# Two transformer blocks on one core: the first squares, one merge, the key-norm sums and two bias loads put at other places in their queues

## The chip, the cores and the metric

The kernel runs on one core of a Trainium2 chip. The metric is the time that one execution takes on the device, in microseconds (us), as the median of three runs. The engines are called as in the profile: PE (TensorE, the matmuls), PEld (its weight loads), DVE (VectorE), ACT (ScalarE), POOL (GpSimd) and SP (SyncE, which here only issues the weight transfers). The engines run side by side, each through its own list of instructions in order, and semaphores tie them together: `wait_ge(s, n)` holds an engine until the semaphore `s` has reached `n`, `then_inc` raises it when an instruction is done.

## What is computed

`reference()` sends 256 tokens of width 1024 through `first_block` and then `second_block`. Cut to the four places that matter here:

```python
y = xf * lax.rsqrt(jnp.mean(xf * xf, axis=-1, keepdims=True) + NORM_EPS)   # rms_norm, then * gain

# first_block, layer 0: gated linear attention (gla_mixer), 4 heads, causal, with a decay per channel
attn = jnp.einsum('bhid,bhjd,bhijd->bhij', qi, ki, decay)
o = rms_norm(o, head_gain) * jax.nn.silu(g)

# first_block, layer 1: differential attention; the keys are normed per half head
kv = rms_norm(h, kv_norm) @ w_kv
k = rms_norm(k.reshape(B, S, DIFF_HEADS, 2, DIFF_DH), k_norm)

# second_block: three branches; the state-space one (ssd) ends in a norm per group of 512 channels,
# the sliding-window attention adds a bias that depends on the distance of two tokens
y = rms_norm_2((y * jax.nn.silu(z)).reshape(b, l, SSD_GROUPS, SSD_INNER // SSD_GROUPS), norm_g)
logits = logits + rel_bias
```

## The kernel before

All matrix products are float32 products made out of parts. A chunk is 128 columns of a weight (all 1024 rows); there are 420 chunks, and SP fetches two at a time (a slab of 1 MB) into a ring of four. ACT copies a chunk rounded into `w_hi` (`cut_hi`, L1199), DVE puts the rest into `w_lo` (`cut_lo`, L1926). The activations are split in the same way into `X.hi` (ACT), `X.lo` (DVE, `operand_lo`, L1939 and L1941) and a bfloat16 copy `X.bf`. PE then takes 16 products of the high weight with the high and the low activation (L469, L470) and 8 of the low weight with the bfloat16 copy (L479). Chunks are cut three ahead (`AHEAD`), and everything is written out by hand: the order of a list is the order of the code in the engine's block. So what comes first where is decided by the loops below alone.

Four places are touched.

**The start.** ACT makes the eight high operands of the first norm's input, DVE the eight low ones. At the same time POOL runs `first_squares`: four squares of pairs (L2679), three sums (L2683) and a last one into `sumsq` (L2686). PE runs chunk 0 and chunk 1 as each low operand comes, then chunk 2, and then `stats(0, ...)` (L557, L560), which needs `sumsq`; the chunk results wait for the scale that comes of it.

**The end of the linear attention.** In a loop over `u`, DVE runs `decayed(u - 1)` (L2077 to L2082, the factors of a unit, from the exponentials of ACT at L1367) and then `merge(u - 2)` (L2090 and L2091, the masked sum of the scores that PE made of the unit before). PE's `scores(7)` (L645, L647) waits for both `decayed(7)` and `merge(6)`.

**The key norms.** Eight chunks (C_DK is 96) make the keys, one head each. For head n: DVE scales it (L1945), ACT squares it (`head_sq`, L1225), PE sums the squares (`head_sums`, L570), ACT turns the sum into a scale (`head_rstd`, L1229 and L1233) and DVE applies it (`head_out`, L1971). PE takes the sum of head n - 1 right behind chunk n.

**The bias loads.** The state-space branch ends in `ssd_norm` (L2414), which raises `s_on`. POOL waits for the last of these, then issues the loads of the bias for the first two units of the window attention (`bias`, L2760), then waits for the operands of the next product and issues the load of `mem` (L2781). DVE's `swa_max` (L2543) needs the bias; ACT's `swa_exp` (L1799) comes behind it, and in ACT's list the square of the next query head (L1695), for which PE's sum (L570) waits.

Of the kernel before, what the change touches and what calls it, by code (L numbers as in the profile page):

```python
# [25 lines left out]
KC = D // P  # L26
# [4 lines left out]
GLA_HEADS, GLA_RANK, GLA_TAU = 4, 16, 16.0  # L31
DIFF_HEADS, DIFF_DH = 8, 64
LAMBDA_INIT = 0.8 - 0.6 * float(np.exp(-0.3))
TAPS, SSD_TAPS = 31, 4
SSD_HEADS, SSD_GROUPS = 32, 4
# [116 lines left out]
def program(nc, w_d, par_d, con_d, gm_d, x_d, mem_d, band_d, out_d):  # L152
    ctx = ExitStack()
    with ctx:
# [41 lines left out]
        XA, XB = XSet("xa"), XSet("xb")  # L196
# [6 lines left out]
        def pcol(name, i=0, n=1):  # L203
            return par[:, PCOL[name] + i:PCOL[name] + i + n]
# [6 lines left out]
        class Cut:  # L211
# [5 lines left out]
            def __call__(self, *shape, rows=P):  # L217
# [6 lines left out]
                if len(shape) == 3:  # L224
# [35 lines left out]
        d_k, d_q = cut(DIFF_HEADS, T), cut(DIFF_HEADS, T)  # L260
# [90 lines left out]
        sa = {n: sem("s_" + n) for n in ("tap", "silu", "z", "dtf", "dts", "dt", "dtx", "dta", "dte", "da", "cs", "bias", "x", "xd", "cb", "cbs", "c", "e",  # L351
                                         "sc", "y", "yd", "sq", "n", "r", "on", "eb", "nx", "gb")}
# [99 lines left out]
        def _(pe):  # L452
# [110 lines left out]
            def head_sums(k):  # L563

                pe.wait_ge(hn_sq, k + 1)
                if k >= 2:
                    pe.wait_ge(hn_ln, k - 1)
                if DIFF_HEADS < k < 2 * DIFF_HEADS or k == HN_K + 1:
                    pe.wait_ge(hn_ln, k)
                mm(head_sums_at(k), bones, hn_sqb[:, k % 2], start=True, stop=True).then_inc(hn_mm, 1)  # L570
# [44 lines left out]
            n = GLA_RANK + 1  # L615
# [110 lines left out]
            for n in range(9):  # L726
                if n == 0:
                    opening_chunk(C_DK, 0, XA, XA_DIFF, C_DK - 8)
                elif n < 8:
                    chunk(C_DK + n, n, XA, None)  # L730
                    if n == 1:
                        stats(2, True, True)
                if n:
                    head_sums(n - 1)

            mm(ps[0:SWA_HEADS, 7, 0:BAND], par[0:33, PCOL["rel"]:PCOL["rel"] + SWA_HEADS], con[0:33, CCOL["oh"]:CCOL["oh"] + BAND],
               start=True, stop=True).then_inc(band_mm, 1)
# [1 line left out]
            def v_or_q(i):  # L739

                if i < 2 * DIFF_HEADS:
                    c = C_DVQ + i
                    if i in Q_AT:
                        chunk(c, c, XB, XB_DQ if i == 0 else None, banks=2)
                    else:
                        token_half(c, XA, None, banks=2)
                if i - 1 in Q_AT:
                    head_sums(DIFF_HEADS + Q_AT.index(i - 1))
# [38 lines left out]

            for i in range(DVQ_AHEAD):
                v_or_q(i)
            pe.wait_ge(bf_set, 2)  # L790
            pe.wait_ge(band_set, 1)
            diff_scores(0)
# [200 lines left out]
            for s in range(R_END):  # L993
                g, i = (s - R_LEAD) // R_GROUP, (s - R_LEAD) % R_GROUP
# [179 lines left out]
        def _(act):  # L1174
# [52 lines left out]
            def head_rstd(k):  # L1227
                act.wait_ge(hn_mm, k + 1)
                A(lnt[:, k % 2], head_sums_at(k), ACT.Ln, bias=eps[:, 0:1], scale=1.0 / 64).then_inc(hn_ln, 1)  # L1229
                act.wait_ge(hn_ln, k + 1)  # L1230
                if k >= 2:
                    act.wait_ge(hn_out, k - 1)
                A(hn_rb[:, k % 2], lnt[:, k % 2], ACT.Exp, scale=-0.5).then_inc(hn_r, 1)  # L1233
# [163 lines left out]
            for n in range(9):  # L1397
                if n < 7:
                    cut_hi(C_DK + n + 1 + AHEAD, C_DK + n + 1 + AHEAD)
                if n == 0:  # L1400
                    rms(2, rstd, rtok)
                if n < 8:
                    A(XB.hi[:, n], H[:, n], ACT.Copy, scale=pcol("b_norm", n)).then_inc(XB.hi_done, 1)
                    head_sq(n, C_DK + n, d_k[:, n])
                if n:
                    head_rstd(n - 1)

            act.wait_ge(da["lam"], 1)
            A(d_lam[:, 2:4], d_lam[:, 0:2], ACT.Exp).then_inc(da["lame"], 1)
# [14 lines left out]
            def v_or_q(i):  # L1424

                c = C_DVQ + i + AHEAD
                if i in Q_AT:
                    cut_hi(c, c)
                elif i % 2 == 0:
                    cut_hi(c, c)  # L1430
                    diff_value(i)
                elif i < 2 * DIFF_HEADS:
                    diff_value(i)
                    cut_hi(c, c)
# [29 lines left out]
            def diff_exp(u):  # L1464
                t = u % 2
                act.wait_ge(da["max"], u + 1)
                if u >= 2:
                    act.wait_ge(da["a"], u - 1)
                for c in range(2):
                    ins = A(d_p[:, u % 2, c, 0:(t + 1) * P], diff_scores_at()[:, c, 0:(t + 1) * P], ACT.Exp,  # L1470
                            bias=d_st[:, u % 2, c:c + 1], accum_out=d_st[:, u % 2, 2 + c:3 + c])
                ins.then_inc(da["p"], 1)

            for i in range(DVQ_AHEAD):
                q_norm(i)
                v_or_q(i)
            diff_exp(0)
            for u in range(2 * DIFF_HEADS):
                h, t = u // 2, u % 2
# [217 lines left out]
            for s in range(R_END):  # L1697
                cut_hi(C_R + s + AHEAD, C_R + s + AHEAD)
                g, i = (s - R_LEAD) // R_GROUP, (s - R_LEAD) % R_GROUP
# [210 lines left out]
        def _(dve):  # L1910
# [57 lines left out]
            def head_out(k, x, gain):  # L1968

                dve.wait_ge(hn_r, k + 1)  # L1970
                STT(x, x, gain, hn_rb[:, k % 2], ALU.mult, ALU.mult).then_inc(hn_out, 1)  # L1971
# [133 lines left out]
                    operand_lo(XB, KC * XB_GLA + 2 * h + half + 1, 2 * h + half, g_og[:, h % 2, half], pcol("a_head_norm", half))  # L2105

            for u in range(2 * GLA_HEADS + 2):
                if 1 <= u <= 2 * GLA_HEADS:
                    decayed(u - 1)
                if u >= 2:  # L2110
                    merge(u - 2)
                if u in (6, 7):
                    gated(u - 6)
                if u < 2 * GLA_HEADS:
                    for c in (8 + 2 * u, 9 + 2 * u):
                        cut_lo(c + AHEAD, c + AHEAD)
                        if c < C_GV:
                            scaled(c, c, g_gate[:, c - C_GG], 2)
                if u == 7:
                    out_lo(0)  # L2120
# [34 lines left out]
            for n in range(10):  # L2155
                if n < 8:
                    cut_lo(C_DK + n + AHEAD, C_DK + n + AHEAD)
                    if n == 0:
                        dve.wait_ge(rstd_done, 3)
                    scaled(C_DK + n, n, d_k[:, n])  # L2160
                    operand_lo(XB, KC * XB_DQ + n + 1, n, H[:, n], pcol("b_norm", n))
                if n >= 2:
                    head_out(n - 2, d_k[:, n - 2], pcol("k_norm"))

            def v_or_q(i):

                if i - 1 in Q_AT:
                    c = C_DVQ + i - 1
                    dve.wait_ge(bank_free, c)
                    scaled(c, c, d_q[:, Q_AT.index(i - 1)], banks=2)  # L2170
                if 0 < i < 2 * DIFF_HEADS:
                    c = C_DVQ + i + AHEAD - 1
                    cut_lo(c, c)

            def q_out(i):

                if i - 3 in Q_AT:
                    h = Q_AT.index(i - 3)
                    head_out(DIFF_HEADS + h, d_q[:, h], gains[:, 2:3])

            for i in range(DVQ_AHEAD):
                v_or_q(i)
                q_out(i)

            dve.wait_ge(da["lame"], 1)
# [28 lines left out]
            for u in range(2 * DIFF_HEADS):  # L2214
# [12 lines left out]
                if u in DIFF_OPERAND_AT:  # L2227
                    i = DIFF_OPERAND_AT[u]
# [60 lines left out]
            for n in range(16):  # L2289
                c = C_CONV + n  # L2290
                i = n // 2
# [361 lines left out]
        def _(pool):  # L2653
# [19 lines left out]

            def first_squares():

                for i in range(4):
                    pool.wait_ge(in_done[i // 2], 16)
                    h = H[:, 2 * i:2 * i + 2]
                    G.tensor_tensor(x_squares[:, min(i, 1)], h, h, ALU.mult).then_inc(sq_step, 1)  # L2679
                    steps[0] += 1  # L2680
                    if i:
                        pool.wait_ge(sq_step, steps[0])
                        G.tensor_tensor(x_squares[:, 0], x_squares[:, 0], x_squares[:, 1], ALU.add).then_inc(sq_step, 1)  # L2683
                        steps[0] += 1
                        pool.wait_ge(sq_step, steps[0])
                G.tensor_tensor(sumsq[:], x_squares[:, 0, 0:T], x_squares[:, 0, T:2 * T], ALU.add).then_inc(sq_step, 2 * KC - 1 - steps[0])  # L2686
                steps[0] = 2 * KC - 1
# [60 lines left out]
                pool.wait_ge(ca["silu"], k + 1)  # L2748
                G.tensor_scalar(XA.bf[:, k], c_out[:, k], one[:, 0:1], None, ALU.mult).then_inc(XA.bf_done, 1)

            pool.wait_ge(sa["on"], 4 * SSD_GROUPS)

            def bias(u):

                p, t = u // 2, u % 2
                nk = (t + 1) * P
                if u >= 2:
                    pool.wait_ge(wa["ss"], u - 1)
                skew = bass.AP(band_d.tensor, 2 * p * BAND + P - 1 + (1 - t) * P, [[SWA_HEADS * BAND - 1, P], [BAND, 2], [1, nk]])
                pool.dma_start(w_bias[:, u % 2, :, 0:nk], skew).then_inc(band_in[u % 2], 16)  # L2760
# [15 lines left out]

            bias(0)
            bias(1)
            pool.wait_ge(XB.bf_done, KC * (XB_Y0 + 1))
            pool.wait_ge(XB.lo_done, KC * (XB_Y0 + 1))  # L2780
            pool.dma_start(x_mem, mem_d).then_inc(mem_in, 16)  # L2781
# [153 lines left out]
```

## Time and profile before

| | |
|---|---|
| median of three runs | 1421.48 us (1421.24 to 1424.57) |
| the profiled execution | 1420.15 us, of which 1418.1 us lie between its first and last instruction |
| PE busy | 1367.4 us, 96% of the span |
| PEld busy | 1260.7 us, 89% |
| DVE busy | 1044.8 us, 74% |
| ACT busy | 890.8 us, 63% |
| POOL busy | 335.1 us, 24% |
| mean granted PE clock | 0.993 of full speed |
| moved from and to memory | 233.8 MB, 165 GB/s on the mean |

The profile is one execution, seen instruction by instruction. Its time is 1.33 us below the median of the runs. A busy share is an average over a program with many stages, so it says who is loaded most, and not what a given stage waits for. That is read from the view of waits (an engine, the line that it could not start, and who released it) and from the timeline of an engine, where each row gives the start, the time taken, the engine, the line, the operation, what it writes and reads, how many alike were merged into the row, and in brackets how long the engine had been idle and what ended that.

### The profile page before, as it was taken

To read this page: it belongs to the slowest core of one execution; us is meant where nothing else is said; L and a number is where in the kernel's file an instruction comes from. 1 tells how busy PE (TensorE), PEld (TensorE's weight loads), DVE (VectorE), ACT (ScalarE), POOL (GpSimd) and SP (SyncE) were. 2 spreads that over 40 slices of the span, in tenths; PEclk is the share of its full clock that TensorE was granted. 3 is DMA by queue.
4 is the path that set the end of the run, shared out by engine and by line. 5 is a ranking of instruction groups with operands and counts; after the bars stand their busy time and mean duration, and the time that the engine had idled before them with its cause. 6 is when DMAs were issued, how large, how long until landed. Compare 5 with 4: busy or idle time off the path is not lost.

```text
span 1418.1 us, 29905 instructions
## 1 busy us (share of the span) xinstructions
PE 1367.4 (96%) x11462; PEld 1260.7 (89%) x11462; DVE 1044.8 (74%) x1570; ACT 890.8 (63%) x1689; POOL 335.1 (24%) x326
## 2 busy tenths in 40 slices
PE   6998999999999999999899999999999999999998
PEld 6997999998888999999888989888788899899998
DVE  6797855567577865568999999867797686666554
ACT  5555744457577554467887878848667565655543
POOL 2000410115001210032855535410411031411110
PEclk9999999999999999999999999999999999999999
DMA  8332565554843555554444444434455454356551
GB/s 321 135 120 90 180 207 182 203 183 146 195 135 118 195 193 195 191 179 161 166 149 150 149 157 142 155 114 138 158 176 176 138 198 149 114 184 199 187 202 66
DMA packets 35608, 233.80 MB, mean 165 GB/s; under 512 B 4000, under 2 KB 7072, under 8 KB 8352
## 3 DMA queue, kind: packets, MB, share of 16 engines
q1 hardware_dynamic: 31104, 223.75, 45.9%
q10 hardware_dynamic: 3216, 4.19, 1.9%
q0 software_dynamic: 1168, 4.20, 1.0%
q8 instruction: 83, 1.36, 0.4%
q14 instruction: 37, 0.30, 0.1%
HBM read 227.93 MB, written 4.19 MB: 164 GB/s over the span
## 4 chain that ended last, share of the span: by engine, by line
PE 75%; DVE 16%; ACT 4%; issue 3%; DMA 0%; DVEq 0%; ACTq 0%; SPq 0%
PE ps L469 12%; PE ps L470 11%; PE ps L479 11%; PE ps L538 7%; PE ps L539 6%; PE ps L544 6%; DVE w_lo L1926 5%; DVE arena L2346 2%; PE ps L880 2%; PE ps L881 2%; PE ps L884 2%; DVE xa_both L1941 2%; PE ps L521 2%; PE ps L522 1%; PE ps L524 1%
## 5 line engine op out<-in xcount | busy, mean ns | idle before, releaser
L1926 DVE TENSOR_TENSOR w_lo<-raw,w_hi 128x1024 bf16<-128x1024 f32 x420 | 548.3, 1308 | 202.1 <-ACT w_hi L1199 201.8
L1199 ACT CAST w_hi<-raw 128x1024 fp32r<-128x1024 f32 x420 | 438.5, 1047 | 304.0 <-PE ps L544 133.8
L469 PE MATMUL ps<-xa_both,w_hi 128*128 128x256 f32 x1296 | 326.3, 293 | 12.0 <-ACT w_hi L1199 10.3
L470 PE MATMUL ps<-xa_both,w_hi 128*128 128x256 f32 x1296 | 309.1, 280 | 0.0
L469 PEld LDWEIGHTS ps<-xa_both,w_hi 128*128 128x128 f32 x1296 | 247.2, 191 | 18.3 <-issue 12.0
L470 PEld LDWEIGHTS ps<-xa_both,w_hi 128*128 128x128 f32 x1296 | 247.7, 191 | 0.5
L538 PE MATMUL ps<-xb_both,w_hi 128*128 128x256 f32 x832 | 204.7, 289 | 0.0
L539 PE MATMUL ps<-xb_both,w_hi 128*128 128x256 f32 x832 | 195.2, 277 | 0.0
L479 PE MATMUL ps<-xa_bf,w_lo 128*128 128x256 bf16 x1296 | 169.4, 274 | 1.2 <-DVE w_lo L1926 1.1
L2705 POOL TENSOR_TENSOR arena<-arena 128x256 f32<-128x256 f32 x96 | 69.7, 727 | 388.7 <-DVE arena L2008 388.7
L538 PEld LDWEIGHTS ps<-xb_both,w_hi 128*128 128x128 f32 x832 | 156.6, 188 | 1.6 <-DVE xb_both L1941 0.2
L539 PEld LDWEIGHTS ps<-xb_both,w_hi 128*128 128x128 f32 x832 | 156.7, 188 | 0.1
L880 PE MATMUL ps<-xb_both,w_hi 128*128 128x256 f32 x592 | 148.0, 293 | 4.4 <-DVE arena L2346 3.0
L881 PE MATMUL ps<-xb_both,w_hi 128*128 128x256 f32 x592 | 139.0, 278 | 0.0
L479 PEld LDWEIGHTS ps<-xa_bf,w_lo 128*128 128x128 bf16 x1296 | 113.8, 98 | 18.6 <-DVE w_lo L1926 2.0
L880 PEld LDWEIGHTS ps<-xb_both,w_hi 128*128 128x128 f32 x592 | 111.4, 188 | 8.2 <-issue 5.9
L881 PEld LDWEIGHTS ps<-xb_both,w_hi 128*128 128x128 f32 x592 | 111.5, 188 | 0.6
L544 PE MATMUL ps<-xb_bf,w_lo 128*128 128x256 bf16 x832 | 108.9, 274 | 0.0
L544 PEld LDWEIGHTS ps<-xb_bf,w_lo 128*128 128x128 bf16 x832 | 73.0, 98 | 10.6
L469 PE MATMUL ps<-xb_both,w_hi 128*128 128x256 f32 x320 | 80.2, 292 | 0.5 <-DVE xb_both L1939 0.4
L884 PE MATMUL ps<-xb_bf,w_lo 128*128 128x256 bf16 x592 | 77.5, 274 | 0.0
L470 PE MATMUL ps<-xb_both,w_hi 128*128 128x256 f32 x320 | 75.8, 279 | 0.0
(350 smaller groups left out, 2368.2 us busy)
## 6 DMA issues: line engine op xcount, KB each, us to landing
raw<-weights SPq DMA_DIRECT2D x210, 1024.0 KB, 4.9
band<-arena ACTq DMA_DIRECT2D x1, 3072.0 KB, 35.6
arena<-band POOLq DMA_DIRECT2D x8, 256.0 KB, 3.2
arena<-gla_masks SPq DMA_DIRECT2D x1, 1088.0 KB, 15.2
H<-x_t SPq DMA_DIRECT2D x2, 512.0 KB, 4.6
arena<-band POOLq DMA_DIRECT2D x8, 128.0 KB, 2.7
arena<-mem_t POOLq DMA_DIRECT2D x1, 1024.0 KB, 5.9
out_t<-H ACTq DMA_DIRECT2D x8, 128.0 KB, 2.0
```

Of the source, the lines that this page charges most:

```text
L469: mm(ps[:, bank, 0:T], w_hi[:, s, k], X.hi[:, k], start=k == 0, stop=False)
L470: mm(ps[:, bank, 0:T], w_hi[:, s, k], X.lo[:, k], start=False, stop=False)
L479: last = mm(ps[:, bank, 0:T], w_lo[:, s, k], X.bf[:, k], start=False, stop=k == KC - 1)
L538: mm(sums(n), w_hi[:, s, i], X.hi[:, k], start=opens, stop=False)
L539: mm(sums(n), w_hi[:, s, i], X.lo[:, k], start=False, stop=False)
L544: done = mm(sums(n), w_lo[:, s, i], X.bf[:, k], start=False, stop=last and (k, n) == DOWN[j][-1] and j >= 4)
L880: mm(ps[:, bank, 0:T], w_hi[:, c % HI_SLOTS, k], XB.hi[:, k], start=k == 0, stop=False)
L881: mm(ps[:, bank, 0:T], w_hi[:, c % HI_SLOTS, k], XB.lo[:, k], start=False, stop=False)
L884: last = mm(ps[:, bank, 0:T], w_lo[:, c % HI_SLOTS, k], XB.bf[:, k], start=False, stop=k == KC - 1)
L1199: nc.scalar.copy(w_hi[:, j % HI_SLOTS].rearrange("p k n -> p (k n)"), raw[:, j // 2 % RING, j % 2]).then_inc(hi_done, 1)
L1926: TT(w_lo[:, j % HI_SLOTS].rearrange("p k n -> p (k n)"), raw[:, j // 2 % RING, j % 2], w_hi[:, j % HI_SLOTS].rearrange("p k n -> p (k n)" ...
L2705: G.tensor_tensor(m_sq[:, j % 2], m_relu[:, j % 2], m_relu[:, j % 2], ALU.mult).then_inc(sq_done, 1)
```

## The change

It moves waits and instructions; no arithmetic is added or left out. POOL's first squares wait until DVE has written all eight low operands. In the last step but one of the linear attention's loop DVE merges unit 6 before it makes the factors of unit 7. In the key loop the sum of head n - 2 instead of head n - 1 follows chunk n on PE, the scale on ACT and its use on DVE move with it, and the last head's sum, scale and use go behind the first query chunk. POOL's wait for the last `ssd_norm` is put behind the first two bias loads, which now wait for the last products and weighted scores of the state-space branch instead.

```diff
             # PE
-                if n:
-                    head_sums(n - 1)
+                if n >= 2:
+                    head_sums(n - 2)
...
             for i in range(DVQ_AHEAD):
                 v_or_q(i)
+                if i == 0:
+                    head_sums(DIFF_HEADS - 1)
...
             # ACT
-                if n:
-                    head_rstd(n - 1)
+                if n >= 2:
+                    head_rstd(n - 2)
...
                 q_norm(i)
                 v_or_q(i)
+                if i == 0:
+                    head_rstd(DIFF_HEADS - 1)
...
             # DVE
             for u in range(2 * GLA_HEADS + 2):
+                if u == 2 * GLA_HEADS:
+                    merge(u - 2)
                 if 1 <= u <= 2 * GLA_HEADS:
                     decayed(u - 1)
-                if u >= 2:
+                if u >= 2 and u != 2 * GLA_HEADS:
                     merge(u - 2)
...
-                if n >= 2:
-                    head_out(n - 2, d_k[:, n - 2], pcol("k_norm"))
+                if n >= 3:
+                    head_out(n - 3, d_k[:, n - 3], pcol("k_norm"))
...
                 v_or_q(i)
+                if i == 1:
+                    head_out(DIFF_HEADS - 1, d_k[:, DIFF_HEADS - 1], pcol("k_norm"))
                 q_out(i)
...
             # POOL
             def first_squares():
+                pool.wait_ge(XA.lo_done, KC)
...
-            pool.wait_ge(sa["on"], 4 * SSD_GROUPS)
+            pool.wait_ge(sa["y"], 2 * SSD_GROUPS)
+            pool.wait_ge(sa["sc"], 4 * SSD_GROUPS)
...
             bias(0)
             bias(1)
+            pool.wait_ge(sa["on"], 4 * SSD_GROUPS)
             pool.wait_ge(XB.bf_done, KC * (XB_Y0 + 1))
```

How the lists stand afterwards, at three places. First PE at the key chunks: L557 and L560 are the row statistics behind key chunk 1, L570 is a head's sum, L469 and L470 open the next chunk. Between the two versions the list differs here by one row:

```order
 L557 MATMUL ps<-sumsq,ones 128x256
 L560 MATMUL ps<-ones,sumsq 128x1 x2
-L570 MATMUL ps<-hn_sqb,con 128x256
 L469 MATMUL ps<-xa_both,w_hi 128x256
 L470 MATMUL ps<-xa_both,w_hi 128x256
```

and it comes back behind the first query chunk (`xb` operands):

```order
 L470 MATMUL ps<-xb_both,w_hi 128x256
 L479 MATMUL ps<-xb_bf,w_lo 128x256 x8
+L570 MATMUL ps<-hn_sqb,con 128x256
 L469 MATMUL ps<-xb_both,w_hi 128x256
 L470 MATMUL ps<-xb_both,w_hi 128x256
```

So chunk 2 follows the statistics at once, each later place of a sum holds the sum of one head earlier, and one sum stands behind the first query chunk.

Second DVE at the end of the linear attention, before (L2077 to L2082 make the factors of unit 7, the first L2090 and L2091 merge unit 6, the second unit 7):

```order
L1941 SCALAR_TENSOR_TENSOR xb_both<-arena,par,xb_both 128x256 [waits xb_hi_done] x2
L2077 TENSOR_TENSOR arena<-arena 128x896 [waits g_e]
L2081 TENSOR_TENSOR arena<-arena 128x128
L2082 TENSOR_TENSOR arena<-arena 128x896
L2090 TENSOR_TENSOR arena<-ps,arena 128x1024 [waits g_m,g_s]
L2091 TENSOR_REDUCE arena<-arena 128x128 [waits dve_step]
L2090 TENSOR_TENSOR arena<-ps,arena 128x1024 [waits g_m,g_s]
```

and in the changed kernel, whose lines stand four further down here (L2094 is the L2090 of before):

```order
L1945 SCALAR_TENSOR_TENSOR xb_both<-arena,par,xb_both 128x256 [waits xb_hi_done] x2
L2094 TENSOR_TENSOR arena<-ps,arena 128x1024 [waits g_m,g_s]
L2095 TENSOR_REDUCE arena<-arena 128x128 [waits dve_step]
L2081 TENSOR_TENSOR arena<-arena 128x896 [waits g_e]
L2085 TENSOR_TENSOR arena<-arena 128x128
L2086 TENSOR_TENSOR arena<-arena 128x896
L2094 TENSOR_TENSOR arena<-ps,arena 128x1024 [waits g_m,g_s]
```

The merge of unit 6 has moved ahead of the three instructions that wait for ACT's exponentials (`g_e`).

Third POOL before the window attention, before (`s_on` is the last norm, `w_ss` the biased scores):

```order
L2749 TENSOR_SCALAR xa_bf<-arena,one 128x256 [waits c_silu] x3
L2760 DMA arena<-band 128x2x128 [waits s_on]
L2760 DMA arena<-band 128x2x256
L2781 DMA arena<-mem_t 128x2048 [waits xb_lo_done,xb_bf_done]
L2760 DMA arena<-band 128x2x128 [waits w_ss]
```

and in the changed kernel:

```order
L2758 TENSOR_SCALAR xa_bf<-arena,one 128x256 [waits c_silu] x3
L2770 DMA arena<-band 128x2x128 [waits s_sc,s_y]
L2770 DMA arena<-band 128x2x256
L2792 DMA arena<-mem_t 128x2048 [waits xb_lo_done,xb_bf_done,s_on]
L2770 DMA arena<-band 128x2x128 [waits w_ss]
```

The order of the transfers is the same; the wait for `s_on` has moved from the first of them to the third.

## Rows read from the trace of the kernel before

**Rows 1.** The page, chain that ended last: shares of the span by engine.

```profile
PE 75%; DVE 16%; ACT 4%; issue 3%; DMA 0%; DVEq 0%; ACTq 0%; SPq 0%
```

**Rows 2.** Waits of PE, whole span: us in total, times, longest us.

```profile
PE ps L570 <- ACT hn_sqb L1225: 3.0, 2, 2.2
```

**Rows 3.** Stretches: us, busy time (count) per engine, granted PE clock, DMA share, GB/s.

```profile
117.70:124.50 6.80, 5.26 (x22) 5.02 (x23) 2.83 (x3) 1.14 (x2) 0.00 (x0) 0.50 0.00 0
336.20:339.60 3.40, 3.40 (x17) 3.32 (x16) 2.44 (x4) 1.98 (x5) 3.40 (x3) 0.50 0.78 294
1005.30:1008.60 3.30, 3.30 (x12) 2.00 (x12) 2.91 (x9) 2.32 (x7) 1.26 (x2) 0.50 0.11 15
```

**Rows 4.** Timeline of the start: DVE, POOL, ACT, PE.

```profile
6.00 9.42 DVE L1941 SCALAR_TENSOR_TENSOR xa_both<-H,par,xa_both 128x256 fp32r<-128x256 f32 x8 [6.00 <-ACT xa_both L1285]
15.35 3.48 DVE L1926 TENSOR_TENSOR w_lo<-raw,w_hi 128x1024 bf16<-128x1024 f32 x3
...
5.44 2.22 POOL L2679 TENSOR_TENSOR arena<-H 128x512 f32<-128x512 f32 x2 [4.20 <-DMA H<-x_t]
14.41 0.73 POOL L2686 TENSOR_TENSOR sumsq<-arena 128x256 f32<-128x256 f32 x1
...
9.13 1.99 ACT L1199 CAST w_hi<-raw 128x1024 fp32r<-128x1024 f32 x2 [0.38 <-DMA raw<-weights]
...
10.28 0.55 PE L469 MATMUL ps<-xa_both,w_hi 128*128 128x256 f32 x1 [10.28 <-ACT w_hi L1199]
16.07 0.42 PE L469 MATMUL ps<-xa_both,w_hi 128*128 128x256 f32 x1
18.63 0.35 PE L469 MATMUL ps<-xa_both,w_hi 128*128 128x256 f32 x1
23.66 0.60 PE L557 MATMUL ps<-sumsq,ones 128*128 128x256 f32 x2
```

**Rows 5.** Timeline of POOL further on: one product beside DVE's work, one later.

```profile
1013.80 1.41 POOL L2771 TENSOR_TENSOR sqtmp<-arena 128x256 f32<-128x256 f32 x1
...
1024.22 0.61 POOL L2771 TENSOR_TENSOR sqtmp<-arena 128x256 f32<-128x256 f32 x1
```

**Rows 6.** Timeline of DVE and PE at the end of the linear attention.

```profile
111.62 1.66 DVE L1941 SCALAR_TENSOR_TENSOR xb_both<-arena,par,xb_both 128x256 fp32r<-128x256 f32 x2 [0.36 <-ACT xb_both L1351]
113.73 1.09 DVE L2077 TENSOR_TENSOR arena<-arena 128x896 f32<-128x896 f32 x1 [0.44 <-ACT arena L1367]
...
115.94 1.22 DVE L2090 TENSOR_TENSOR arena<-ps,arena 128x1024 f32<-128x1024 f32 x1
117.19 1.91 DVE L2091 TENSOR_REDUCE arena<-arena 128x128 f32<-128x1024 f32 x1
...
112.06 0.39 PE L647 MATMUL ps<-arena 128*128 128x128 f32 x2
...
119.24 3.33 PE L645 MATMUL ps<-arena 128*128 128x128 f32 x14 [3.83 <-DVE arena L2091]
```

**Rows 7.** Timeline of PE and ACT at the key chunks.

```profile
335.69 0.75 PE L570 MATMUL ps<-hn_sqb,con 128*128 128x256 f32 x2 [2.23 <-ACT hn_sqb L1225]
...
340.53 0.60 PE L570 MATMUL ps<-hn_sqb,con 128*128 128x256 f32 x2
...
343.74 0.60 PE L570 MATMUL ps<-hn_sqb,con 128*128 128x256 f32 x2
...
335.22 0.42 ACT L1225 ACTIVATE hn_sqb<-arena 128x256 f32<-128x256 f32 x1 [0.16 <-DVE arena L1945]
```

**Rows 8.** Timeline of PE, POOL and DVE at the first bias loads.

```profile
978.74 0.44 PE L954 MATMUL ps<-con,arena 128*64 128x128 f32 x4
...
999.22 1.62 POOL L2760 DMA_DIRECT2D arena<-band  x2 [42.33 <-DVE arena L2414]
...
1002.04 0.43 DVE L2543 SCALAR_TENSOR_TENSOR arena<-ps,arena 128x256 f32<-128x256 f32 x1 [0.93 <-DMA arena<-band]
...
1005.07 1.11 PE L570 MATMUL ps<-hn_sqb,con 128*128 128x256 f32 x2 [2.72 <-ACT hn_sqb L1695]
```

## The prediction

> **What bounds the kernel now.** I read the chain that ended last first: three quarters of it are PE's own work [rows 1], so time can only be won where PE stands still or runs at the lower clock. Next come the waits of PE, where the reader looks for the lines that the change touches: the key heads' sums (L570, released by ACT's L1225) cost 3.0 us in two waits, the longer 2.2 [rows 2]; the others stand in brackets in the timelines. Third, the granted clock by stretches. Three of these four places are followed, or one is filled, by a stretch at 0.50, which is 1.2 instead of 2.4 GHz: 6.8 us at the end of the linear attention, 3.4 at the key chunks, 3.3 at the bias loads [rows 3]. A wait there costs its length and then some more. Last, the timelines of the four places, for who is late.
>
> **The squares at the start.** DVE's eight low operands end at 15.42, 9.42 us for eight, and POOL's chain runs from 5.44 to 15.14 at the same time [rows 4]. PE's first 16 matmuls go from 10.28 to 16.07, 5.79 us, since most of them wait for a low operand; the next twelve go from 16.07 to 18.63, 0.213 each, and 16 at that pace are 3.41 [rows 4]. So 2.4 us are lost there, and PE could be at the statistics (23.66) at 21.3 at best. In the change POOL starts when the low operands are done. ACT's high halves, which they need, end at 8.75 (the cast behind them starts at 9.13 after 0.38 of idle time [rows 4]). Elsewhere two low operands take 1.66 us, 0.83 each [rows 6], so the last is done by 9.6; with POOL silent it should be quicker, and I take 9.4, an estimate.
>
> What is then late is the squares themselves: PE's L557 needs `sumsq`. From 9.4, POOL needs its old 9.7 us and now meets DVE's four splits of the weights (1.16 each [rows 4]), because the first casts are done at 11.1 [rows 4]. A POOL product beside such a split took 1.41 and without one 0.61 [rows 5], 0.8 more; four of these make 3.2. So the squares end at 9.4 + 9.7 + 3.2 = 22.3, and the statistics run at 22.3 instead of 23.66: **1.4 gained**. Bounds: without any slowing the squares end at 19.1, PE decides, and it is 2.4. If POOL stands for the whole of the four splits and the small one behind them, some 1.2 each, they end at 25.1 and 1.4 are lost. I take the middle, by the row that shows just this pair of engines.
>
> The rule that speaks against this edit is in the Trainium skill, "SBUF — State Buffer", section "SBUF: two separate sides": a VectorE operation with two inputs in SBUF and a GpSimd operation that reads SBUF lock each other out, and whichever starts first keeps the shared ports for its whole instruction. The trace agrees as to the direction [rows 5]. By that rule each split holds POOL back for its full length, which is the bound of 25.1 and a loss of 1.4; by the rows' pace it is 22.3.
>
> **One merge first.** DVE is free at 113.28 (111.62 + 1.66), and idles 0.44 until ACT's exponentials let L2077 start at 113.73; the scores of unit 6 that the merge needs are done at 112.45 [rows 6]. In the new order the merge (115.94 to 119.10, 3.16) starts at once, and the factors (113.73 to 115.94, 2.21) follow it without a wait, their exponentials being done by then. PE's L645 then starts at 113.28 + 3.16 + 2.21 = 118.65 instead of 119.24, some of which is the semaphore's way: I take **0.5 gained**. PE stays idle for 3.3 us. The low stretch of 6.8 us is twice as long as the two others [rows 3], and PE works through only its last 5.3 us. If PE's earlier return ended it at the others' length, the 3.4 us that fall away give half of that, 1.7, back; so the bounds are 0 and 2.2.
>
> **The key sums one chunk later.** The first sum waits 2.23 and starts at 335.69, when ACT's square (335.22 + 0.42) is just done [rows 7]. Now chunk 2 runs in that time, about 333.3 to 336.1, and its sum finds the square done at 335.64. The 2.23 go, and so does the reason for the low clock from 336.2 to 339.6 [rows 3]: from 335.69 to 340.53, one sum and one chunk take 4.84 us, the next sum and chunk to 343.74 take 3.21 [rows 7], which is 1.63 more. The second wait (3.0 - 2.2 = 0.8 [rows 2]) belongs to the last head, whose sum moves behind the first query chunk; it goes too. Together 2.2 + 1.6 + 0.8: **4.7 gained**. The moved scale on ACT and the use on DVE run under PE's next chunk, 2.8 us, in which each has one cast or split and three small steps. If the clock falls all the same, 3.0 are left; the upper bound is 5.0, as the 0.3 of the sum itself also moves out of the slow stretch.
>
> **The bias loads.** POOL issues them at 999.22, after a wait of 42.33 for DVE's norm; the last product of the state-space branch that they now need ends at 979.18 (978.74 + 0.44) [rows 8]. Nothing of POOL stands between, and the load of `mem` behind them keeps its old wait. The bias is then there long before DVE's `swa_max`, which now starts 0.93 late, at 1002.04 [rows 8]. The instructions up to PE's L570 at 1005.07 hang on it one by one, so its wait of 2.72 becomes 1.8: **1.0 gained**, with the 0.93 rounded up. What is late next is ACT's square, behind the exponentials in its list. If the shorter wait no longer brings the clock down (1005.3 to 1008.6 at 0.50 [rows 3]), up to half of these 3.3 us comes on top, 2.6 in all; if DVE's other work takes the gap, nothing is gained.
>
> **Sum.** 1.4 + 0.5 + 4.7 + 1.0 = 7.6 us off the profiled execution of 1420.15, so 1412.55. That execution stands 1.33 below the median of 1421.48, so against the median the forecast is **1413.9**. No edit adds an instruction, and what follows each place hangs on semaphores, so it comes earlier with it.
>
> **Rivals.** A measurement of this kernel can tell 0.3% from no change, which is 4.3 us: faster means under 1417.2.
>
> *The squares become the late wait.* POOL is held back fully; the start loses 1.4 instead of gaining it: -4.8, 1416.7. For it: DVE's splits come one behind another there. Against: 1.41 and not 1.8 in [rows 5].
>
> *The clock gives more.* The start is bound by PE (2.4), the stretch at 119 gets shorter (2.2), the one at 1005 goes (2.6): with 4.7 it is -11.9, 1409.6; half of the extra gives 1411.7. For it: all three low stretches follow PE waits that get shorter. Against: two of these waits stay at 1.8 and 3.3 us.
>
> *Low clocks stay and the small ones miss.* The clock at the key chunks still falls (3.0), the start and the merge give nothing, the bias 1.0: -4.0, 1417.5, no change. It includes that the change doesn't do what it says at the start or at the merge.
>
> *Slower, by the clock.* Each low stretch of 3.4 us costs 1.63 [rows 7]. All later waits of PE shift by up to 7.6 us, and short ones that left the clock up may then bring it down. From five new stretches on (7.6 / 1.63 = 4.7) the gain is gone; with eight (13.0) it is 5.4 slower, 1426.9. Against: the waits are not longer than before, and only their place in time shifts.
>
> **How the numbers follow.** Forecast 0.56, more from the clock 0.22, late squares 0.12, no change 0.07, slower 0.03. The range takes in the first three and leaves the last two out: from 1409.5, just under the whole of the extra, to 1417.0, just over the late squares. Faster is 0.56 + 0.22 + 0.12 = 0.90, same 0.07, slower 0.03.
>
> **What would show it.** The low operands end by about 9.5 and `sumsq` near 22.3; if it ends after 23.7, the first step is wrong. L645 starts some 6.2 us after the last L647 of the unit before ends, where it was 6.8 (112.45 to 119.24). No wait of L570 for L1225 is left and the clock stays at 1.00 at the key chunks; a new wait at a sum, or a cast that comes late, would break the largest step. `swa_max` no longer waits for a DMA, and L570 behind it waits about 1.8. If all four are seen and the time is not near 1413.9, then waits behind them have grown, and the step "comes earlier with it" is the wrong one.

## The result, and the profile after

The changed kernel takes 1411.56 us (median of 5 runs, 1410.91 to 1414.28), the kernel before 1421.48. The ratio is 0.9926, with a 95% interval from 0.9916 to 0.9937: 9.9 us or 0.74% faster. The forecast was 1413.9 with a range from 1409.5 to 1417.0, so range and direction held, and 2.3 us were won that the sum did not have. Between the two profiled executions the sum is nearly met: it said 1412.55 there, and 1412.25 was measured. The forecast took over the distance of 1.33 between the profile of before and its median; the changed kernel's profile lies 0.69 above its own median, and the two distances make up 2.0 of the 2.3.

First the waits of PE in the changed kernel (us in total, times, longest):

```profile
PE ps L570 <- ACT hn_sqb L1699: 3.4, 2, 1.7
PE ps L645 <- DVE arena L2086: 3.2, 1, 3.2
PE ps L557 <- POOL sumsq L2695: 1.7, 1, 1.7
PE ps L758 <- ACT arena L1472: 1.5, 1, 1.5
PE ps L1088 <- DVE arena L2566: 1.3, 2, 0.9
```

The key sums' waits of [rows 2] have no row any more. The wait at the bias loads fell from 2.72 [rows 8] to 1.7 (the other 1.7 of the first row is the untouched one at 960), and that of L645 from 3.83 [rows 6] to 3.2. One wait is new: PE stands 1.7 us for the squares. The wait of L758 is the old one, and will matter below.

Then the timeline of the changed kernel at the four places, in the columns of the rows above; lines are numbered up to 11 higher here:

```profile
5.98 3.28 DVE L1945 SCALAR_TENSOR_TENSOR xa_both<-H,par,xa_both 128x256 fp32r<-128x256 f32 x8 [5.98 <-ACT xa_both L1287]
...
9.34 3.02 POOL L2688 TENSOR_TENSOR arena<-H 128x512 f32<-128x512 f32 x2 [8.10 <-DVE xa_both L1945]
12.44 2.14 POOL L2692 TENSOR_TENSOR arena<-arena 128x512 f32<-128x512 f32 x1
21.42 0.72 POOL L2695 TENSOR_TENSOR sumsq<-arena 128x256 f32<-128x256 f32 x1
...
13.84 0.41 PE L469 MATMUL ps<-xa_both,w_hi 128*128 128x256 f32 x1
14.23 0.28 PE L469 MATMUL ps<-xa_both,w_hi 128*128 128x256 f32 x1
22.20 0.70 PE L557 MATMUL ps<-sumsq,ones 128*128 128x256 f32 x2 [1.72 <-POOL sumsq L2695]
...
110.74 0.39 PE L647 MATMUL ps<-arena 128*128 128x128 f32 x2
117.29 3.36 PE L645 MATMUL ps<-arena 128*128 128x128 f32 x14 [3.20 <-DVE arena L2086]
...
334.55 0.60 PE L570 MATMUL ps<-hn_sqb,con 128*128 128x256 f32 x2
337.70 0.60 PE L570 MATMUL ps<-hn_sqb,con 128*128 128x256 f32 x2
...
971.75 1.62 POOL L2770 DMA_DIRECT2D arena<-band  x2 [22.67 <-PE ps L956]
...
996.25 0.70 PE L570 MATMUL ps<-hn_sqb,con 128*128 128x256 f32 x2 [1.68 <-ACT hn_sqb L1699]
```

The low operands are done at 9.26 and the squares at 22.14, so the statistics run 1.46 us earlier than in [rows 4]. The key sums follow one another in 3.15 us from the first on, where the first pair was 4.84 apart [rows 7]. The bias loads go out 27 us earlier than in [rows 8].

Last the stretches, in the columns of [rows 3]:

```profile
116.60:123.40 6.80, 6.11 (x24) 5.75 (x25) 2.89 (x3) 1.07 (x3) 0.00 (x0) 0.50 0.01 2
331.80:337.60 5.80, 5.80 (x51) 5.52 (x51) 5.79 (x10) 5.29 (x12) 5.80 (x4) 1.00 0.91 340
372.90:376.30 3.40, 3.38 (x27) 2.80 (x28) 3.22 (x10) 1.98 (x8) 0.00 (x0) 1.00 1.02 419
997.30:1000.60 3.30, 2.90 (x15) 2.38 (x12) 3.23 (x9) 2.17 (x7) 1.26 (x2) 0.50 0.29 60
```

The stretches behind the merge and behind the bias loads are still at 0.50. The key chunks run at 1.00. The third row is a place that the prediction did not look at: right behind L758's wait of 1.5 us. In the kernel before, the same piece of the program stood at 0.50:

```profile
380.60:384.00 3.40, 3.40 (x17) 3.33 (x16) 3.03 (x7) 3.06 (x9) 0.00 (x0) 0.50 1.02 422
```

Where the gain comes from can be read by pairing the products of both kernels one by one and taking the difference of their starts. The changed kernel is 1.4 us ahead behind the statistics, 1.6 after the linear attention, 6.0 at the second key sum, 6.6 behind the last one, 8.1 at 384 us of the kernel before, 8.6 behind the bias loads, 8.3 some 20 us later and 8.0 at the end. The profiled executions are 7.9 apart (1420.15 and 1412.25); the medians 9.9. In these two executions the key sums and L758 give 6.5 where the sum had 4.7 for the key sums, and smaller losses at the other places use up most of that surplus.

### The profile page after: what moved, and what is told of

Read it like the earlier page. It is cut to its first block, busy times and chain, and to the rows that moved or that the text cites. A ratio compares the mean times of both kernels' runs of the same rounds, so it can differ in the third digit from the quotient of the medians.

```text
span 1410.2 us, 29907 instructions
## 1 busy us (share of the span) xinstructions
PE 1362.8 (97%) x11462; PEld 1257.2 (89%) x11462; DVE 1042.2 (74%) x1570; ACT 890.7 (63%) x1689; POOL 338.6 (24%) x326
## 4 chain that ended last, share of the span: by engine, by line
PE 75%; DVE 16%; ACT 4%; issue 3%; POOL 1%; DMA 0%; DVEq 0%; ACTq 0%; SPq 0%; POOLq 0%
PE ps L469 12%; PE ps L470 11%; PE ps L479 11%; PE ps L538 7%; PE ps L539 6%; PE ps L544 6%; DVE w_lo L1930 5%; DVE arena L2354 2%; PE ps L882 2%; PE ps L883 2%; PE ps L886 2%; PE ps L521 1%; PE ps L522 1%; PE ps L524 1%; DVE xa_both L1945 1%
## 5 line engine op out<-in xcount | busy, mean ns | idle before, releaser
L469 PE MATMUL ps<-xa_both,w_hi 128*128 128x256 f32 x1296 | 323.2, 291 | 10.9 <-ACT w_hi L1201 10.3
L470 PE MATMUL ps<-xa_both,w_hi 128*128 128x256 f32 x1296 | 306.5, 278 | 0.0
L469 PEld LDWEIGHTS ps<-xa_both,w_hi 128*128 128x128 f32 x1296 | 245.5, 189 | 16.4 <-issue 12.0
L470 PEld LDWEIGHTS ps<-xa_both,w_hi 128*128 128x128 f32 x1296 | 245.5, 189 | 0.5
L469 PE MATMUL ps<-xb_both,w_hi 128*128 128x256 f32 x320 | 81.0, 294 | 0.5 <-DVE xb_both L1943 0.4
L470 PE MATMUL ps<-xb_both,w_hi 128*128 128x256 f32 x320 | 76.5, 280 | 0.0
```

Of the source, the lines that this page charges most:

```text
L469: mm(ps[:, bank, 0:T], w_hi[:, s, k], X.hi[:, k], start=k == 0, stop=False)
L470: mm(ps[:, bank, 0:T], w_hi[:, s, k], X.lo[:, k], start=False, stop=False)
```

## The experiments

**Each edit alone.** What is to be told apart is whether the extra belongs to one edit or to chance. The four edits, cut to the line that says them:

```diff
 # only_squares
             def first_squares():
+                pool.wait_ge(XA.lo_done, KC)
 # only_merge
+                if u == 2 * GLA_HEADS:
+                    merge(u - 2)
 # only_keys
-                if n:
-                    head_sums(n - 1)
+                if n >= 2:
+                    head_sums(n - 2)
 # only_bias
-            pool.wait_ge(sa["on"], 4 * SSD_GROUPS)
+            pool.wait_ge(sa["y"], 2 * SSD_GROUPS)
+            pool.wait_ge(sa["sc"], 4 * SSD_GROUPS)
...
             bias(1)
+            pool.wait_ge(sa["on"], 4 * SSD_GROUPS)
```

> Only the first edit: POOL's squares start behind the eight low operands. Theory A (each edit is worth its own wait and the low-clock stretch right behind it, and the 2.3 us beyond the forecast are chance of the clock elsewhere): statistics at about 22.2 instead of 23.7, a gain of 1.4, so some 1420.1 us. Theory B (an edit also takes low-clock stretches away further on, by moving later waits in time): 1 to 2 us more than that in the median, 1418 to 1419. Rival of the first step: if the exclusion by the weights' splits cost each split in full, no gain, 1421.5 or later.

> Only the second edit: unit 6 is merged ahead of the factors of unit 7. Theory A: L645's wait of 3.83 shrinks by 0.5 to 0.6, but part of that is given back in the low-clock stretch behind it: 0.3 to 0.5 gained, 1421.0 to 1421.2, not to be told from no change. Theory B: the stretch of 6.8 us at the low clock becomes shorter in some runs, 1 to 2 us gained, 1419.5 to 1420.5.

> Only the third edit: the sums of the key heads one chunk later, the last head's behind the first query chunk. Theory A: both waits of L570 for L1225 and the low-clock stretch at the key chunks go, 4.7 to 5.0 gained, 1416.5 to 1416.8. Theory B: the low-clock stretch near 380 us, which is missing in the profile of the changed kernel, goes by this edit too: 6.3 to 6.6 gained, 1415.0.

> Only the fourth edit: the first two bias loads ahead of the last norm. Theory A: the 0.93 of DVE's wait for the load goes, L570's wait falls from 2.7 to 1.7, of which the low-clock stretch behind it gives back a part: 0.5 to 1.0 gained, 1420.5 to 1421.0. Theory B: that stretch itself goes in a share of the runs, 1.5 to 2.6 gained, 1419 to 1420.

Against 1421.5 for the kernel before on the same chip:

| edit alone | median, us | gain | ratio, 95% interval | forecast's term |
|---|---|---|---|---|
| squares | 1419.82 | 1.7 | 0.9973 to 0.9991 | 1.4 |
| merge | 1420.90 | 0.6 | 0.9982 to 1.0 | 0.5 |
| key sums | 1415.08 | 6.4 | 0.9938 to 0.9966 | 4.7 |
| bias | 1420.35 | 1.2 | 0.9974 to 0.9997 | 1.0 |

The gains add up to 9.9, which is the whole change. Three lie within 0.3 of their terms, and the merge by itself can't be told from no change. The key sums are the term that was mis-sized, as theory B had it for them: by 1.7 of the 2.3. For the other three, theory A's prices are the nearer ones in the medians. In the profile of the key sums alone, the stretch behind L758's wait stands at full clock:

```profile
375.30:378.70 3.40, 3.38 (x28) 2.79 (x29) 3.22 (x9) 2.01 (x8) 0.00 (x0) 1.00 1.01 418
```

The profiles of two other edits, one of each, show that these reach stretches too. With the squares alone, PE's new wait for them (1.9 us) is followed by a low stretch, at which 1.6 us are lost again, and the stretch behind L645's wait is 3.4 us long instead of 6.8:

```profile
23.90:27.30 3.40, 3.40 (x18) 2.93 (x17) 2.33 (x4) 3.34 (x5) 0.00 (x0) 0.50 0.78 320
119.50:122.90 3.40, 3.40 (x16) 3.40 (x17) 0.00 (x0) 0.00 (x0) 0.00 (x0) 0.50 0.00 0
```

Of the four profiles of this study with the squares moved and L645's wait left idle, three have it so short (the first profile of the changed kernel has 6.8); in all seven with the squares at their old place it is 6.8. With the bias edit alone no low stretch follows L570's shorter wait, as theory B had it:

```profile
1006.40:1009.70 3.30, 2.64 (x17) 1.91 (x18) 2.74 (x9) 2.57 (x7) 1.26 (x2) 1.00 0.04 5
```

There 1.9 us are gained in this profile, and 1.4 of them are lost again by 1032, most of it at the wait of L1086 (below). In all seven profiles with the bias loads at their old place a low stretch follows the wait, and in three of the seven with them moved.

**Keeping the wait, but not the idling.** Is it the clock that makes up the rest of the key sums' gain? Here PE does useless products while it waits (the expectations call them idle products); their result is overwritten by the sum.

```diff
+            def fill(at, n, X):
+                for i in range(n):
+                    mm(at, X.hi[:, i % KC, 0:P], X.hi[:, i % KC], start=True, stop=True)
...
+                if n == 1:
+                    fill(head_sums_at(0), 18, XA)
                 if n:
                     head_sums(n - 1)
```

> The kernel before with 18 idle products (operands of the current chunk, result overwritten by the sum itself) put in front of the first key head's sum; the wait of 2.23 us stays, but PE is busy in 2.1 of it. The third edit alone gained 6.4 in the median where its local terms are 2.2 + 1.6 + 0.8. Theory A (the clock falls because PE stands still there, and costs 1.6): the first sum starts at the same time, no low stretch follows, 1.6 gained, 1419.9 us. Theory B (the clock's share is larger than one profile showed, 3 us or more, since the low stretch is longer or a second one follows in other executions): 3 gained, 1418.5. Rival C (the 1.6 is no matter of the clock but of the order of the work): no gain, 1421.5.

It took 1419.15 against 1421.47, a ratio of 0.9980 (0.9971 to 0.9989): 2.3 gained without any wait removed. PE's timeline there:

```profile
334.27 2.39 PE L565 MATMUL ps<-xa_both 128*128 128x256 f32 x18
336.64 0.70 PE L574 MATMUL ps<-hn_sqb,con 128*128 128x256 f32 x2
...
339.90 0.38 PE L574 MATMUL ps<-hn_sqb,con 128*128 128x256 f32 x1
```

From the first sum to the second it takes 3.26 us instead of 4.84 [rows 7]: 1.6, the very term of the sum. So theory A is right on the place, rival C is out, and the median stands between A and B. In the profile the stretch behind L758's wait is gone here as well, although that wait is as long as ever (1.5 us):

```profile
378.90:382.30 3.40, 3.38 (x27) 2.80 (x28) 3.22 (x10) 2.00 (x8) 0.00 (x0) 1.00 1.02 418
```

**The stretch behind L758's wait.** The same trick there, in the kernel before and then in that with the third edit alone:

```diff
             def diff_scores(u):
...
                 pe.wait_ge(hn_out, DIFF_HEADS + h + 1)
+                if u == 1:
+                    fill(ps[:, 3, 0:T], 12, XA)
                 if u:
                     pe.wait_ge(da["p"], u)
```

> The kernel before with 12 idle products in front of the second score of the differential attention, where PE waits 1.52 us for ACT and a low-clock stretch of 3.4 us followed in the profile of before (380.6), but in those of the whole change and of the third edit alone none. Theory A (that stretch is there in a part of the executions only, by where the wait lies in time, and its absence in the changed kernel is chance): 0.5 to 1.5 gained, 1420.0 to 1421.0. Theory B (it is there in all executions of before, and the third edit removes it for good): 1.5 or more in every run, below 1420.0.

In the kernel before it gained 2.5: 1418.96 against 1421.47, ratio 0.9981 (0.9972 to 0.9990), with nine of the eleven runs below 1420.0 and the other two at 1420.0 and 1420.2. So that stretch costs something in most executions. That it is there in all of them, as theory B had it, is not shown, and 2.5 is more than the 1.5 that one such stretch costs in the profiles; where the rest comes from is open.

> The third edit alone (1415.1 us) together with the 12 idle products in front of the second score, which gained 2.5 on the kernel before. Theory A (removing the wait at the key chunks also keeps the clock up at the wait of 1.52 some 40 us later, which is why the third edit gained 6.4 and not 5): nothing left to gain there, 1414.7 to 1415.5. Theory B (the two have nothing to do with each other, and the profiles of the third edit lacked that stretch by chance): 1.5 to 2.5 gained, 1412.6 to 1413.6.

With the third edit it gained nothing: 1415.28 (ratio 0.9957, 0.9942 to 0.9972) beside 1415.08 without the products. That is theory A's result: with the third edit there is nothing left to win at this stretch. The profiles say the same. Of the four profiles in which PE stood still at the first key sum with L758's wait left idle (before, squares, merge, bias), three show a low stretch behind L758. Of the seven profiles in which PE worked there, by the third edit or by the useless products, and with the same idle wait of 1.5 us, none does. So the two go together in ten of these eleven profiles; why is not shown. One reading is left untested: in the three with a low stretch L758's wait begins 38.05 to 38.35 us after the clock has come up again at the key chunks, in the fourth (squares) 39.07. The fall at the key chunks may thus act only by setting when the next wait comes, and no run moved that alone.

**The changed kernel once more.**

> The changed kernel as it is, once more, beside the others on one chip. Theory A (its 9.9 us are the sum of the four edits, 1.7 + 0.6 + 6.4 + 1.2, and its executions differ by where low-clock stretches fall): 1411 to 1412.5, and in its profile no stretch at the key chunks nor at 373, one or two of those at 116, 454 and 997. Theory B (the first result was a lucky draw): 1413 to 1414, the forecast's sum.

1410.59 (1409.76 to 1412.82), against 1422.17 for the kernel before beside it; ratio 0.9929 (0.9912 to 0.9946). Theory A again, a little below its range. Its profile lacks the stretches at the key chunks and at L758, and has the other three, where theory A had one or two. It is 1.6 us ahead of the first profile of the same kernel, of which 1.3 come at the end of the linear attention, where the low stretch was 3.4 us long and not 6.8. So an unchanged kernel differs by this much from one execution to the next.

**Squares behind four low operands.**

```diff
             def first_squares():
 
-                pool.wait_ge(XA.lo_done, KC)
+                pool.wait_ge(XA.lo_done, KC // 2)
```

> The changed kernel, but POOL's squares wait for the first four low operands instead of all eight. In the changed kernel the squares run from 9.34 to 22.1 beside DVE's splits, and PE waits 1.72 for them. Theory A (DVE and POOL take turns; what counts is how long the DVE instruction is that POOL meets, 0.4 for a low operand and 1.2 for a split): POOL starts at about 7.6, the last four low operands come at 13.1 at the latest, in time for PE, the squares end near 20.5 and the wait goes: 1 to 1.7 gained on the changed kernel, 1410. Theory B (POOL's own length decides, 12.7 us from wherever it starts, or PE loses at the late low operands what it wins): within 0.5 of the changed kernel, 1411.5.

1407.43 (four runs, 1407.25 to 1408.35), ratio to the kernel before 0.9902 (0.9887 to 0.9917): the best kernel of the study, and all its runs lie below all eleven of the changed kernel. The timeline of its start:

```profile
5.86 5.87 DVE L1945 SCALAR_TENSOR_TENSOR xa_both<-H,par,xa_both 128x256 fp32r<-128x256 f32 x8 [5.86 <-ACT xa_both L1287]
...
7.62 2.40 POOL L2688 TENSOR_TENSOR arena<-H 128x512 f32<-128x512 f32 x2 [6.37 <-DVE xa_both L1945]
19.21 0.73 POOL L2695 TENSOR_TENSOR sumsq<-arena 128x256 f32<-128x256 f32 x1
...
20.00 0.69 PE L557 MATMUL ps<-sumsq,ones 128*128 128x256 f32 x2
```

POOL's chain is hardly shorter (12.3 us from 7.62 to 19.94, beside 12.8 from 9.34), so theory A's reason, short instructions of DVE instead of long ones, is worth half a microsecond at most. What pays is the earlier start, which costs PE nothing: the last low operand comes at 11.73, still before PE needs it. The statistics run at 20.00 instead of 22.20 without a wait. More followed than theory A had: 3.4 us ahead after the linear attention, whose low stretch was 3.4 us long instead of 6.8 in the profile, and 4.9 at the end, against the first profile of the changed kernel. The shorter stretch is not this edit's doing alone: the second profile of the changed kernel had it too, and was 1.3 ahead by it.

**Products in front of the scores of unit 7.**

```diff
             attend(2)
+            fill(ps[:, 5, 0:T], 26, XA)
             scores(2 * GLA_HEADS - 1)
```

> The changed kernel with 26 idle products in front of the scores of unit 7, where PE still waits 3.20 us; 3.05 of it are then busy. Theory A (the low stretch of 6.8 us behind it comes of the standing still, and half of what PE does in it, 5.3 us of work before, is lost): the scores start at the same time, the clock stays up, 2.5 to 3 gained on the changed kernel, some 1409. Theory B (the clock was down for another reason): no gain, 1411.5.

The clock stays up, and the scores take 1.83 us instead of 3.36:

```profile
116.90:123.50 6.60, 6.43 (x53) 6.00 (x53) 4.42 (x5) 1.43 (x4) 0.20 (x1) 1.00 0.01 2
```

On the spot that gives 2.8 us (0.1 ahead of the changed kernel before it, 2.9 behind it), as theory A had it; in the median only 0.9, at 1410.68 (0.9910 to 0.9938 of before), and nothing against the changed kernel's second median of 1410.59. So no gain of the whole is shown. In its profile 1.2 are given back at a low stretch at 882, which the changed kernel does not have, and 1.1 between 998 and 1022.

> The changed kernel with the squares behind the first four low operands (1407.4) and with the 26 idle products in front of the scores of unit 7. If the clock's fall behind that wait costs here what it cost in the profile (3.4 us at 0.50, 1.5 lost): 1 to 2 gained on 1407.4, 1405.5 to 1406.4. If the low stretch just appears elsewhere, as it partly did in the changed kernel with these products: 1407.

> As the run before, and the 12 idle products in front of the second score too. If the third edit has already taken the low stretch there away: the same as without them, 1405.5 to 1406.4. If not: 1 to 2 less.

1407.91 (0.9893 to 0.9927) and 1407.64 (0.9888 to 0.9921), neither to be told from 1407.43. The first has no low stretch at all between its start and its end:

```profile
core 0: 1405.8 us, clock 1.000
```

Beside the profile without these products it is 1.5 us ahead at 996 and has lost 2.1 by 1020. The waits of its PE show where, with one row that has grown (us in total, times, longest):

```profile
PE ps L1093 <- DVE arena L2571: 2.3, 3, 1.5
```

This is the wait of L1088 in the changed kernel. In the kernel before and with the bias edit alone, PE's timeline has it as

```profile
1029.77 0.66 PE L1086 MATMUL ps<-con,arena 128*128 128x128 f32 x4 [0.57 <-DVE arena L2558]
```

and

```profile
1006.42 0.70 PE L570 MATMUL ps<-hn_sqb,con 128*128 128x256 f32 x2 [1.67 <-ACT hn_sqb L1695]
...
1031.64 0.66 PE L1086 MATMUL ps<-con,arena 128*128 128x128 f32 x4 [1.55 <-DVE arena L2558]
```

There DVE makes the window attention's weights beside POOL's squares of `mem`, and is behind. The longest such wait is 1.56 us in one profile, and two profiles (the squares alone, and the key sums with the products at L758) have none, so what is won ahead of it can be lost in it. What decides its length (how DVE's and POOL's instructions fall beside each other, perhaps) was not tried.

## Why the prediction was right, and where it was short

*Squares (1.4).* Right in the time, and in what becomes late; that the time came out so well is luck in part. The low operands end at 9.26 (9.4 said), the squares at 22.14 (22.3), the statistics move by 1.46. The sum was POOL's old 9.7 us and 0.8 for each of four splits. In the profile four of POOL's operations take 1.0 to 1.1 longer than the 1.04 of a square that starts ahead of a split, 4.3 in all; the chain of 12.8 would be 8.5 without them, an estimate. So the price of a split was too low, and the old 9.7 too long a base, since it already held waits for the low operands. In the changed kernel the two engines take turns:

```profile
18.10 2.06 DVE L1930 TENSOR_TENSOR w_lo<-raw,w_hi 128x1024 bf16<-128x1024 f32 x1
...
14.66 1.04 POOL L2688 TENSOR_TENSOR arena<-H 128x512 f32<-128x512 f32 x1
17.99 1.09 POOL L2688 TENSOR_TENSOR arena<-H 128x512 f32<-128x512 f32 x1
19.15 2.12 POOL L2692 TENSOR_TENSOR arena<-arena 128x512 f32<-128x512 f32 x1
```

The square at 17.99 ends at 19.08, the split 1.08 us after it at 20.16, and the sum 1.11 us after that at 21.27. The rule of the Trainium skill ("SBUF — State Buffer", section "SBUF: two separate sides") is that of such a pair the one that starts first keeps the shared ports for its whole instruction, while the other stands. The trace agrees with it here in size too: each instruction ends about its own length behind the one that it met. The bound of 25.1 was no price of that rule, as it put five holds of 1.2 on the old chain.

The step "PE could be at the statistics at 21.3 at best" was wrong: the gaps in PE's work had also held the clock down. Matmuls take 0.28 from 14.23 on, and in the kernel before from 18.8 on. PE was ready at 20.48 and waited 1.72 (0.9 in the second profile, where the clock rose later, at 16.0), and squares behind four low operands bring the statistics to 20.00.

*Merge (0.5).* Right on the spot: from the end of the last L647 to L645 it takes 6.16 us instead of 6.79. A part goes back, since the low stretch behind it, again 6.8 us long, then covers more work: 0.3 are left behind it in the profile. In the medians the edit alone can't be told from no change.

*Key sums (4.7).* Right as far as the place goes, and the step that was short. On the spot 5.0 are gained, the upper bound: 4.4 up to the second sum (3.8 forecast) and 0.6 at the last head (0.8 forecast). The 1.6 for the clock was shown by itself with the useless products. What the sum lacked is the low stretch 44 us further on, behind a wait that the change does not touch. The prediction held the clock's cost to be a matter of the stretch right behind a wait; here it is 1.5 us more at a second one, and the edit alone gained 6.4.

*Bias loads (1.0).* Right on the spot: DVE's wait for the load is gone, L570's fell by 1.04, and 1.2 in the median for the edit alone. "What follows comes earlier with it" holds only in part, as 0.3 to 1 us are given back at L1088. The low stretch behind the wait, which the sum left in place, is gone in four of the seven profiles with this edit.

*The rivals.* The time lies nearest to "the clock gives more" at half its extra, 1411.7, and only in part for its reasons. In both profiles of the changed kernel the stretch behind the bias loads stayed; the one behind the merge stayed at 6.8 us in the first and fell to 3.4 in the second; and the one that went for good, behind L758, was on no list. No low stretch was new in these two profiles. But the squares alone show that "slower, by the clock" had something to stand on: in their profile a low stretch follows the new wait, as none does in the changed kernel, and another at 891 is not in the profile of before.

## What to carry to other kernels

A wait of TensorE is priced with the low-clock stretch behind it; those behind the next waits, some tens of microseconds on, can go or come with it, as one did here 44 us further on: go through the whole list of low stretches, and ask of each which wait brought it. Where work of POOL is moved out of DVE's way, look at what DVE does next, and try the point halfway: here half the operands were enough, and the other half were in time anyway. A gain is kept only until the next place where another engine sets the pace, so an extra at the clock can vanish there altogether.

## What the runs showed that was not expected

Useless products in a wait keep the clock up, and pay on the spot: 1.6 us at the key sums, 2.8 at the scores of unit 7. In the median of the whole that was 2.3 at the key sums and nothing clear at unit 7. The kernel that has squares behind four low operands and such products runs at a mean clock of 1.000 in its profile, and was no faster (1407.9) than without them at 0.996 (1407.4), as PE then waited longer for DVE further on.

The waits at L758 (1.52) and L645 (3.20 or 3.83, by the order of the merge) are the same to 0.01 us in all profiles that leave them idle, while the low stretch behind L758 comes and goes and that behind L645 lasts 3.4 or 6.8 us. Between the two profiles of the changed kernel, 1.6 us apart, that accounts for 1.3; whether it is the whole scatter of some 3 us between its executions was not shown.
